# State-space mixer of an encoder layer: one segment sum and one weight matrix for both directions, double buffers, and a quarter of the out projection placed ahead of the norm

## The chip, the cores and the metric

One core of a Trainium2 chip runs the whole program. The metric is the device time of one execution in microseconds (us), here the median of several runs. Five engines work side by side, each through its own list of instructions: TensorE (PE, with its weight loads PEld), VectorE (DVE), ScalarE (ACT), GpSimd (POOL) and SyncE (SP, which starts transfers). They wait for each other on semaphores. SBUF is the main memory on the chip, PSUM (eight banks of 128 x 512 fp32) takes the results of TensorE. One fp32 matmul appears as two records in the trace.

## What is computed

An encoder of two layers over 512 tokens of width 1024. The first layer mixes the tokens by an HGRN2 recurrence and by a Mamba-2 state-space (SSD) mixer, joins both in one out projection, and then has a SwiGLU block; the second layer has an S5 mixer and a mixture of experts. The change lies in the SSD mixer and behind it. In the reference:

```python
def _ssd_one_direction(x, dt, a, bm, cm):
    ...
    acum = jnp.cumsum(dtc * a.reshape(g, hg), axis=2)
    ...
    seg = acum[:, :, :, None] - acum[:, :, None, :]
    decay = _masked_exp(mask, seg)
    cb = jnp.einsum('bclgn,bcsgn->bclsg', cc, bc)
    w = cb[..., None] * decay * dtc[:, :, None]
    y_diag = jnp.einsum('bclsgh,bcsghp->bclghp', w, xc)
    to_end = jnp.exp(acum[:, :, -1:] - acum) * dtc
    states = jnp.einsum('bclgn,bclghp->bcghpn', bc, to_end[..., None] * xc)
    ...
    y_off = jnp.einsum('bclgn,bcghpn->bclghp', cc, prev) * jnp.exp(acum)[..., None]
    return (y_diag + y_off).reshape(b, s, h, p)
```

It is called once forward and once on the flipped sequence. `d_skip` times x is added, the result is multiplied by silu(z), normalised by its mean square per group and joined with the HGRN2 output in front of `@ w_out`. There are 4 chunks of 128 tokens, 8 heads of 64 columns, 2 groups and a state of 128.

## The kernel before, in words

The program is written as one list per engine, and the order in each list is fixed by hand. Around the change the order is this.

The last projection products (`dense_fill`, L1350, handed out by `fill_to`) run on TensorE among the last pieces of the HGRN2 part; ScalarE drains their banks (L1961). VectorE runs the HGRN2 norm (`hg_finish`, L2527 reciprocal, L2529 product, L2531) and the convolution of eight blocks of columns (`convolve`, L2545 and L2549), ScalarE its silu (L2010).

Then TensorE makes the cumulative sums of dt·a by products with triangular matrices (L1431, L1432), and ScalarE their exponentials (`ex`, L2006). TensorE transposes the convolved x and B to tokens by columns (L1442), and VectorE copies these out of PSUM (L2615, L2616). GpSimd makes the weights to the chunk's end (`toend`, L1028) and x times them (`xe`, L1035, two buffers), TensorE the six state products (L1449), VectorE the running states (`Hst`; L2627 a copy, L2631 and L2633 a multiply and an add).

For each chunk c then, through one set of buffers:
- TensorE: C·B of the two groups into bank 2 (L1461); the segment sums of 8 heads and 2 directions as four products of 512 columns into banks 4 to 7 (L1468), from `dtaU`, the decays under a triangular mask (LE and GE are the two masks), which GpSimd makes (L1043).
- ScalarE: the exponential of all four banks, 128 x 2048, into `Ew` (L2016).
- VectorE: C·B under both masks (`cbm`, L2637), and `Ew` times it in four products of 128 x 512 (L2645).
- GpSimd: x times dt for both directions (`xdt`, L1049).
- TensorE: for each head and direction a product of `Ew` with `xdt`, 64 columns wide, into bank 3 (L1478, 32 records), and C times the states into banks 0 and 1 (L1484).
- VectorE: d_skip times x (L2649), the state parts scaled and added (L2654, L2656), bank 3 added (L2658), times silu(z) (L2661). ScalarE takes the squares (`ssd_squares`, L769).

After the last chunk come the square root (ScalarE, L2022), its reciprocal and the scaling (VectorE, L2663, L2668), the transposes (TensorE, L1492), and their copies into `mixT` (VectorE, L2672). Rows 0 to 3 of `mixT` hold the HGRN2 output, rows 4 to 7 the SSD output. `dense("o0", mixT)` and `dense("o1", mixT)` are the out projection, 32 matmuls each (L1179); the loop over `kk` takes rows 0 to 3 first and then 4 to 7. VectorE adds the result to the residual stream (L2680).

## Time and profile before

| | us |
|---|---|
| median of 3 runs | 2890.85 (2890.79 to 2893.72) |
| the profiled execution, its own time | 2891.91 |
| its span in the trace | 2890.1 |
| TensorE busy | 2564.2 (89%) |
| VectorE, ScalarE, GpSimd busy | 1696.9, 1250.9, 224.6 |
| first cumulative sum starts (L1431) | 452.92 |
| first exponential of segments (L2016) | 481.91 |
| out projection (L1179) | 569.15 to 624.37 |

The times of the trace count from the span's start. The profiled execution took 1.06 us longer than the median. A page of the profile gives busy times and shares; single instructions, waits and the chain that ended last come from the trace. "Clock" is the share of full speed that TensorE was granted.

### The profile page before, as it was taken

The page shows a single profiled execution, that of the slowest core. Times are in us where ns is not written, and L with a number is a line of the kernel's source. Part 1 is how long each engine was busy: PE and PEld are TensorE (multiplying, and loading weights), DVE is VectorE, ACT ScalarE, POOL GpSimd, SP SyncE. Part 2 cuts the span into 40 slices and gives each one's busy share as a digit, 9 for nine tenths or more (in the row PEclk, how much of TensorE's full clock was granted, in tenths as well). Part 3 has the DMA queues.
Part 4 walks back from the last instruction along what each step waited for, and adds up shares of the span by engine and source line. Part 5 has one row for each costly group of instructions (what it writes and reads, how often), then busy time and mean ns, then how long its engine had stood idle before and what let it go on. Part 6 is the DMA issues. An engine that isn't in the chain of part 4 may idle for free.

```text
span 2890.1 us, 31325 instructions
## 1 busy us (share of the span) xinstructions
PE 2564.2 (89%) x12573; PEld 2059.7 (71%) x12573; DVE 1696.9 (59%) x1883; ACT 1250.9 (43%) x1352; POOL 224.6 (8%) x235
## 2 busy tenths in 40 slices
PE   4989896789999997586977999999999999999977
PEld 2445564548888785486767988899779988898853
DVE  5697785422222333257336668776886778667852
ACT  2343422112222222254224657656666567556741
POOL 3003733100000000000000000000000000000010
PEclk9999988699999998757977999999999999999989
DMA  8446410013233232532317779976997789876960
GB/s 230 141 146 193 120 59 30 7 58 103 88 102 100 76 101 73 142 117 105 122 37 264 238 252 373 319 252 239 337 348 254 249 288 369 271 253 238 373 220 29
DMA packets 317023, 528.70 MB, mean 183 GB/s; under 512 B 19302, under 2 KB 175562, under 8 KB 314218
## 3 DMA queue, kind: packets, MB, share of 16 engines
q1 hardware_dynamic: 287690, 481.83, 48.9%
q0 software_dynamic: 6000, 26.27, 2.8%
q10 hardware_dynamic: 23184, 18.55, 2.0%
q8 instruction: 101, 1.65, 0.2%
q14 instruction: 48, 0.39, 0.0%
HBM read 497.05 MB, written 47.91 MB: 189 GB/s over the span
## 4 chain that ended last, share of the span: by engine, by line
PE 79%; DVE 9%; ACT 4%; issue 3%; POOL 3%; DMA 2%; SPq 0%; ACTq 0%; DVEq 0%; POOLq 0%
PE psum L1653 25%; PE psum L1281 15%; PE psum L1712 11%; PE psum L1513 5%; PE psum L1714 4%; PE psum L1179 4%; PE psum L1202 3%; PE psum L1570 2%; DVE stages_r L2909 1%; PE psum L1350 1%; PE psum L1589 1%; ACT stages_r L2153 1%; PE psum L1478 1%; POOL stages L1020 1%; DVE stages L2267 1%
## 5 line engine op out<-in xcount | busy, mean ns | idle before, releaser
L2909 DVE TENSOR_TENSOR stages_r<-kept,stages_r 128x2048 fp32r<-128x2048 f32 x336 | 769.3, 2291 | 272.6 <-ACT stages_r L2153 271.9
L1653 PE MATMUL psum<-stages_r 128*128 128x512 f32 x3136 | 749.4, 398 | 21.0 <-DVE stages_r L2964 11.1
L2153 ACT ACTIVATE stages_r<-kept 128x2048 fp32r<-128x2048 f32 x336 | 637.4, 1912 | 264.7 <-PE psum L1653 138.1
L1653 PEld LDWEIGHTS psum<-stages_r 128*128 128x128 f32 x3136 | 591.5, 191 | 148.9 <-DVE stages_r L2909 12.4
L1712 PE MATMUL psum<-stages_r 128*128 128x320 f32 x1792 | 465.8, 346 | 6.3 <-issue 3.2
L1281 PE MATMUL psum<-stages_r 128*128 128x512 f32 x1920 | 442.0, 393 | 17.2 <-DVE stages_r L2688 17.2
L1281 PEld LDWEIGHTS psum<-stages_r 128*128 128x128 f32 x1920 | 364.6, 190 | 94.0 <-issue 17.7
L1714 PE MATMUL psum<-stages_r 128*128 128x160 f32 x1792 | 423.6, 236 | 0.0
L1714 PEld LDWEIGHTS psum<-stages_r 128*128 128x128 f32 x1792 | 343.4, 192 | 2.0
L1712 PEld LDWEIGHTS psum<-stages_r 128*128 128x128 f32 x1792 | 337.7, 188 | 9.0 <-DVE stages_r L2909 3.8
L2688 DVE TENSOR_TENSOR stages_r<-kept,stages_r 128x2048 fp32r<-128x2048 f32 x54 | 123.6, 2293 | 362.6 <-ACT stages_r L2033 362.6
L2033 ACT ACTIVATE stages_r<-kept 128x2048 fp32r<-128x2048 f32 x54 | 103.1, 1915 | 349.1 <-PE psum L1281 245.1
L1513 PE MATMUL psum<-stages_r,stages_front_r 128*128 128x512 f32 x672 | 154.6, 393 | 6.8 <-DVE stages_front_r L2707 6.8
L1513 PEld LDWEIGHTS psum<-stages_r,stages_front_r 128*128 128x128 f32 x672 | 127.5, 190 | 33.9 <-issue 7.2
L1202 PE MATMUL psum<-stages,kept 128*128 128x512 f32 x256 | 119.1, 611 | 0.8 <-ACT stages L1815 0.8
L1179 PE MATMUL psum<-kept,stages 128*128 128x512 f32 x256 | 110.4, 593 | 1.6 <-ACT stages L1815 0.8
L2189 ACT ACTIVATE stages<-stages 128x160 f32<-128x160 f32 x112 | 37.8, 337 | 158.3 <-DVE stages L2941 158.3
L1179 PEld LDWEIGHTS psum<-kept,stages 128*128 128x128 f32 x256 | 48.5, 190 | 62.3 <-issue 60.3
L1086 POOL DMA_INDIRECT stages<-moe_rows_by_token,stages x8 | 18.3, 2292 | 892.6 <-PE psum L1661 522.4
L1202 PEld LDWEIGHTS psum<-stages,kept 128*128 128x128 f32 x256 | 47.2, 193 | 54.9 <-issue 53.9
L2944 DVE TENSOR_TENSOR kept<-stages 128x160 f32<-128x160 f32 x112 | 36.7, 327 | 45.2 <-ACT stages L2189 45.2
L1156 PE MATMUL psum<-kept,stages 128*128 128x128 f32 x160 | 26.1, 334 | 39.2 <-DVE stages L2267 39.0
(378 smaller groups left out, 2547.4 us busy)
## 6 DMA issues: line engine op xcount, KB each, us to landing
kept<-in_moe_w_gu_dram SPq DMA_DIRECT2D x224, 1024.0 KB, 6.2
kept<-in_moe_w_down_dram SPq DMA_DIRECT2D x112, 1024.0 KB, 6.1
kept<-in_ffn_w_gu_dram SPq DMA_DIRECT2D x28, 1024.0 KB, 5.2
kept<-in_ev_w_in_dram SPq DMA_DIRECT2D x16, 1024.0 KB, 6.7
kept<-in_ffn_w_down_dram SPq DMA_DIRECT2D x14, 1024.0 KB, 5.0
s_output_maps_by_state<-stages ACTq DMA_DIRECT2D x64, 128.0 KB, 2.0
s_input_maps<-stages ACTq DMA_DIRECT2D x32, 256.0 KB, 2.5
s_output_maps<-s_output_maps_by_state SPq DMA_DIRECT2D x32, 256.0 KB, 4.9
```

The source lines that it names most:

```text
L1179: m = pe.matmul(psum[:, b0 + b, 0:width], act[:, 4 * kk + k, b * P:(b + 1) * P], w[:, k, 0:width], **at)
L1202: m = pe.matmul(psum[:, b, :], *pair, start=kk == 0 and k == 0, stop=kk == 1 and k == 3)
L1281: m = pe.matmul(psum[:, 4 * (g % 2) + b, :], *pair, start=kk == 0 and k == 0 and n == 0, stop=kk == 1 and k == 3 and n == 2, skip_group_ch ...
L1513: m = pe.matmul(psum[:, 2 * c + hf, :], a[:, k, at], w[hf][:, k, :], start=j == 0 and k == 0 and n == 0, stop=j == FJ - 1 and k == 3 and n ...
L1570: m = pe.matmul(psum[:, b % 8, (2 * gl + e) * NC5:(2 * gl + e + 1) * NC5], w[:, 4 * i + gl, e, :], U[:, 8 * q + 4 * i + gl, :], start=True ...
L1653: m = pe.matmul(out_, a, b, start=start and n == 0, stop=stop and n == len(pairs) - 1, skip_group_check=True)
L1712: pe.matmul(bank[:, 0:2 * CAP], wh[:, k, fs], x_[:, k, :], start=k == 0, stop=False, skip_group_check=True)
L1714: m = pe.matmul(bank[:, 0:CAP], wl[:, k, fs], x_[:, k, 0:CAP], start=False, stop=k == 7, skip_group_check=True)
L2033: act.activation(f_high[t % 2], ring[:, n % RING, :].rearrange("p (k n) -> p k n", k=4), ACT.Copy).then_inc(s_wh, 1)
L2153: act.activation(w_high[n % WSLOTS], unit_tile(n), ACT.Copy).then_inc(s_wh, 1)
L2688: dve.tensor_tensor(f_low[t % 2], ring[:, (SPLIT_RUNS[run][1] + t) % RING, :].rearrange("p (k n) -> p k n", k=4), f_high[t % 2], ALU.subtr ...
L2909: dve.tensor_tensor(w_low[n % WSLOTS], unit_tile(n), w_high[n % WSLOTS], ALU.subtract).then_inc(s_ws, 1)
```

## The change

- **One segment sum for both directions.** The products for the forward and the backward direction accumulate in the same two banks; a pair of tokens lies in one triangle or in the other. The exponential is 128 x 1024 instead of 128 x 2048.
- **One weight matrix.** `Ew` is multiplied by C·B straight from PSUM (two products of 128 x 512), then by `dtw` (one of 128 x 1024). `dtw` holds dt of the forward direction under LE plus dt of the backward direction under GE; GpSimd builds it for each chunk with a multiply of 128 x 1024 and, per half, a multiply and an add of 128 x 512. The y products are then 8 matmuls (16 records), on x itself; `xdt` and `cbm` are gone. C·B is made for two chunks at a time.
- **Two buffers.** `Ew`, `dtaU`, `dtw`, `ytmp` and the banks of the segment sums are double, `xe` has six buffers. VectorE's outputs add bank 3 ahead of the state parts, so that the banks come free earlier.
- **Moved work.** The cumulative sums go ahead among the last projection products; the copies of x and B go from VectorE to ScalarE; `toend` and `xe` from GpSimd to VectorE; the HGRN2 norm of the last head goes behind the last convolution block; the state products come in another order (the forward direction first).
- **Out projection.** `dense` takes a list of halves. The HGRN2 half of `o0`, 16 matmuls, comes ahead of the transposes of the normed output, which now use banks 0 and 1; its other half and `o1` come behind them.

The diff, cut to this, with its indentation reduced:

```diff
+ytmp = [ssa.take(512) for _ in range(2)]
+Ew = [ssa.take(1024).rearrange("p (k t) -> p k t", t=P) for _ in range(2)]
...
-xe = ssa.take(1024).rearrange("p (d n) -> p d n", d=2)
...
+dtw = [ssa.take(1024).rearrange("p (k t) -> p k t", t=P) for _ in range(2)]
...
-Ew = ssa.take(2048).rearrange("p (d n t) -> p d n t", d=2, t=P)
-dtaU = ssa.take(2048).rearrange("p (d n t) -> p d n t", d=2, t=P)
+dtaU = [ssa.take(2048).rearrange("p (d n t) -> p d n t", d=2, t=P) for _ in range(2)]
+dtw_half = ssa.take(512).rearrange("p (k t) -> p k t", t=P)
...
-SSD_STATES = [(0, 0), (1, 3), (0, 1), (1, 2), (0, 2), (1, 1)]
+SSD_STATES = [(0, 0), (0, 1), (0, 2), (1, 3), (1, 2), (1, 1)]
+SSD_ENDS = [(0, 0), (0, 1), (1, 1), (0, 2), (1, 2), (1, 3)]
+SSD_SEG = lambda c: psum[:, 4 + 2 * (c % 2):6 + 2 * (c % 2), :]
+SSD_TURN = lambda c: (2, 6)[c % 2]
...
+    def masked_decays(c):
+        if c >= 2:
+            pool.wait_ge(s_seg, c - 1)
         for d in range(2):
...
+            m = pool.tensor_tensor(dtaU[c % 2][:, d, :, :], (LE, GE)[d].unsqueeze(1).broadcast_to([P, MH, P]),
                                    dta[:, d, c, :].unsqueeze(2).broadcast_to([P, MH, P]), ALU.mult)
         m.then_inc(s_dtau, 1)
...
-            m = pool.tensor_tensor(xdt[:, d, :].rearrange("p (k n) -> p k n", k=MH),
...
+    def masked_steps(c):
+        if c == 1:
+            pool.wait_ge(s_conv, CB)
+            pool.wait_ge(s_cact, 1)
+        if c >= 2:
+            pool.wait_ge(s_w, c - 1)
+        if c:
+            pool.wait_ge(s_dtw, c)
+        out_ = dtw[c % 2]
+        chain.link(pool.tensor_tensor(out_, LE.unsqueeze(1).broadcast_to([P, MH, P]),
+                                      dts[:, 0, c, :].unsqueeze(2).broadcast_to([P, MH, P]), ALU.mult))
+        for g in range(2):
+            at = slice(MH // 2 * g, MH // 2 * (g + 1))
+            chain.link(pool.tensor_tensor(dtw_half, GE.unsqueeze(1).broadcast_to([P, MH // 2, P]),
+                                          dts[:, 1, c, at].unsqueeze(2).broadcast_to([P, MH // 2, P]), ALU.mult))
+            chain.settle()
+            m = pool.tensor_tensor(out_[:, at, :], out_[:, at, :], dtw_half, ALU.add)
...
+        m.then_inc(s_dtw, 1)
+    pool.wait_ge(s_dt, 1)
+    pool.wait_ge(s_o, HEADS)
+    pool.wait_ge(s_gram, 2 * PAIR_SLOTS)
+    masked_decays(0)
+    masked_decays(1)
+    pool.wait_ge(s_X, UNITS)
+    masked_steps(0)
+    masked_steps(1)
+    for c in range(2, TC):
+        masked_decays(c)
+        masked_steps(c)
...
-    def dense(name, act):
+    def dense(name, act, halves=(0, 1)):
...
+        if g >= 2 and 0 in halves:
             all_drained(groups[g - 2][0])
...
+        for kk in halves:
...
+    fill_to(rest + 4)
...
+    pe.matmul(psum[:, 0, 128:192], ones, dta.rearrange("p d c k -> p (d c k)"), start=True,
+              stop=True).then_inc(s_cum, 1)
     hg_squares(2)
     fill_to(rest + 9)
     hg_squares(3)
     fill_to(rest + TAIL)
...
+    pe.wait_ge(s_mix, HEADS - 1)
...
     for c in range(TC):
...
+        b = SSD_TURN(c)
         if c >= 2:
...
         m.then_inc(s_xt, 1)
+    pe.wait_ge(s_ex, 1)
     for m_, (d, c) in enumerate(SSD_STATES):
...
+        pe.wait_ge(s_xtd, c + 1)
+        pe.wait_ge(s_xe, SSD_ENDS.index((d, c)) + 1)
...
         for g in range(GROUPS):
             m = pe.matmul(psum[:, m_ % 2, g * 256:(g + 1) * 256], btok[:, c, g * P:(g + 1) * P],
...
+                          xe[SSD_ENDS.index((d, c))][:, g * 256:(g + 1) * 256], start=True, stop=True)
         m.then_inc(s_st, 1)
...
+    pe.wait_ge(s_xe, 6)
     pe.wait_ge(s_cact, CB)
...
+    pe.wait_ge(s_mix, HEADS)
+    def segments(c):
+        pe.wait_ge(s_dtau, c + 1)
+        if c >= 2:
+            pe.wait_ge(s_E, c - 1)
+        for n in range(2):
+            for d in range(2):
+                m = pe.matmul(SSD_SEG(c)[:, n, :], (GT, LT)[d],
+                              dtaU[c % 2][:, d, 4 * n:4 * n + 4, :].rearrange("p k t -> p (k t)"),
+                              start=d == 0, stop=d == 1)
+        m.then_inc(s_seg, 1)
+    def cb_products(pair):
+        if pair:
+            pe.wait_ge(s_w, 2)
+        for c in (2 * pair, 2 * pair + 1):
...
+            for g in range(GROUPS):
...
+                m = pe.matmul(psum[:, 2, o:o + P], xc[:, 4 + g, at], xc[:, 6 + g, at], start=True, stop=True)
+        m.then_inc(s_cb, 1)
+    def ssd_outputs(c):
         at = slice(c * P, (c + 1) * P)
...
+        if c == 0:
+            pe.wait_ge(s_H, 6)
+        else:
             pe.wait_ge(s_yd, c)
...
         for d in range(2):
...
             for g in range(GROUPS):
                 m = pe.matmul(psum[:, d, g * 256:(g + 1) * 256], xc[:, 6 + g, at],
                               Hst[d][:, c - 1 + d, g * 256:(g + 1) * 256], start=True, stop=True)
+        pe.wait_ge(s_w, c + 1)
+        for k in range(MH):
+            m = pe.matmul(psum[:, 3, k * MP:(k + 1) * MP], Ew[c % 2][:, k, :], xst[:, c, k * MP:(k + 1) * MP],
+                          start=True, stop=True)
         m.then_inc(s_y, 1)
+    segments(0)
+    cb_products(0)
+    segments(1)
+    ssd_outputs(0)
+    segments(2)
+    cb_products(1)
+    ssd_outputs(1)
+    segments(3)
+    ssd_outputs(2)
+    ssd_outputs(3)
+    dense("o0", mixT, (0,))
     for c in range(TC):
         pe.wait_ge(s_yn, c + 1)
+        pe.wait_ge(s_yd, TC)
         if c >= 2:
             pe.wait_ge(s_ym, c - 1)
         for q in range(4):
-            m = pe.transpose(psum[:, 4 + c % 2, q * P:(q + 1) * P], yst[:, c, q * P:(q + 1) * P], ident)
+            m = pe.transpose(psum[:, c % 2, q * P:(q + 1) * P], yst[:, c, q * P:(q + 1) * P], ident)
         m.then_inc(s_yt, 1)
     pe.wait_ge(s_ym, TC)
-    dense("o0", mixT)
+    dense("o0", mixT, (1,))
...
+    act.wait_ge(s_cum, 1)
+    act.activation(ex, psum[:, 0, 0:192], ACT.Exp).then_inc(s_ex, 1)
...
+    def conv_silu(cb):
         act.wait_ge(s_conv, cb + 1)
         act.activation(xc[:, cb, :], conv[cb], ACT.Silu, bias=parT[:, 40 + cb:41 + cb]).then_inc(s_cact, 1)
+    def xs_copies(c):
+        act.wait_ge(s_xt, c + 1)
+        b = SSD_TURN(c)
+        act.activation(xst[:, c, :], psum[:, b, :], ACT.Copy)
+        act.activation(btok[:, c, :], psum[:, b + 1, 0:256], ACT.Copy).then_inc(s_xtd, 1)
+    for cb in range(4):
+        conv_silu(cb)
+    fill_drain(late[-1])
+    for cb in range(4, 7):
+        conv_silu(cb)
+    xs_copies(0)
+    conv_silu(7)
+    for c in range(1, TC):
+        xs_copies(c)
     act.activation(zs, zs, ACT.Silu).then_inc(s_zact, 1)
     for c in range(TC):
         act.wait_ge(s_seg, c + 1)
...
+        if c >= 2:
+            act.wait_ge(s_y, c - 1)
+        act.activation(Ew[c % 2].rearrange("p k t -> p (k t)"), SSD_SEG(c).rearrange("p b n -> p (b n)"),
                        ACT.Exp).then_inc(s_E, 1)
...
+        if c >= 2:
...
     convolve(CB - 2)
-    hg_finish(3)
     convolve(CB - 1)
...
-        dve.tensor_copy(xst[:, c, :], psum[:, b, :])
...
+    chain.link(dve.tensor_tensor(toend.rearrange("p d c k -> p (d c k)"), ex[:, 64:128],
...
+    chain.settle()
+    hg_finish(3)
+    def chunk_state(m_):
+        d, c = SSD_STATES[m_]
         dve.wait_ge(s_st, m_ + 1)
...
+        if m_ % 3 == 0:
             dve.tensor_copy(new, bank).then_inc(s_H, 1)
         else:
...
+            dve.wait_ge(s_H, m_)
...
             chain.settle()
...
     for c in range(TC):
...
+        for n, (d, c_) in enumerate(SSD_ENDS):
+            if c_ == c:
+                dve.tensor_tensor(heads(xe[n]), heads(xst[:, c, :]), by_head(toend[:, d, c, :]),
+                                  ALU.mult).then_inc(s_xe, 1)
+        if c:
+            chunk_state(c - 1)
+    for m_ in range(3, 6):
+        chunk_state(m_)
+    def chunk_weights(c):
+        dve.wait_ge(s_cb, c // 2 + 1)
         dve.wait_ge(s_E, c + 1)
...
+        w = Ew[c % 2]
+        for g in range(GROUPS):
+            e = w[:, HPG * g:HPG * (g + 1), :]
+            cb = psum[:, 2, (2 * (c % 2) + g) * P:(2 * (c % 2) + g + 1) * P]
+            chain.link(dve.tensor_tensor(e, e, cb.unsqueeze(1).broadcast_to([P, HPG, P]), ALU.mult))
+        dve.wait_ge(s_dtw, c + 1)
+        chain.settle()
+        dve.tensor_tensor(w, w, dtw[c % 2], ALU.mult).then_inc(s_w, 1)
+    def chunk_outputs(c):
...
         dve.wait_ge(s_xtd, c + 1)
...
+        chain.link(dve.tensor_tensor(heads(y), heads(xst[:, c, :]), by_head(dskip), ALU.mult))
         dve.wait_ge(s_y, c + 1)
         dirs = [d for d in range(2) if c != (0, TC - 1)[d]]
         for d in dirs:
...
+            chain.link(dve.tensor_tensor(heads(ytmp[d]), heads(psum[:, d, :]), by_head(exA[:, d, c, :]), ALU.mult))
         chain.settle()
         dve.tensor_tensor(y, y, psum[:, 3, :], ALU.add).then_inc(s_yd, 1)
         dve.wait_ge(s_yd, c + 1)
+        for d in dirs:
+            chain.link(dve.tensor_tensor(y, y, ytmp[d], ALU.add))
+            chain.settle()
...
         dve.tensor_tensor(y, y, zs[:, c, :], ALU.mult).then_inc(s_yz, 1)
+    chunk_weights(0)
+    chunk_weights(1)
+    chunk_outputs(0)
+    chunk_weights(2)
+    chunk_outputs(1)
+    chunk_weights(3)
+    chunk_outputs(2)
+    chunk_outputs(3)
```

**TensorE, one inner chunk.** Before, for the second chunk (L1461 is C·B, L1468 segment sums, L1478 y products, L1484 state parts):

```order
L1461 MATMUL psum<-stages 128x128 [waits cb_masked]
L1461 MATMUL psum<-stages 128x128
L1468 MATMUL psum<-stages,kept 128x512 [waits segment_exp_ready,dta_masked]
L1468 MATMUL psum<-stages,kept 128x512 x3
L1478 MATMUL psum<-stages 128x64 [waits ssd_y_drained,x_dt_ready,ssd_weights_ready]
L1478 MATMUL psum<-stages 128x64 x15
L1484 MATMUL psum<-stages 128x256 x4
```

Now, the same stretch (L1485 segment sums of the third chunk, L1498 C·B of the third and fourth, L1512 state parts and L1516 y products of the second):

```order
L1485 MATMUL psum<-stages,kept 128x512 [waits segment_exp_ready,dta_masked]
L1485 MATMUL psum<-stages,kept 128x512 x3
L1498 MATMUL psum<-stages 128x128 [waits ssd_weights_ready]
L1498 MATMUL psum<-stages 128x128 x3
L1512 MATMUL psum<-stages 128x256 [waits ssd_y_drained]
L1512 MATMUL psum<-stages 128x256 x3
L1516 MATMUL psum<-stages 128x64 [waits ssd_weights_ready]
L1516 MATMUL psum<-stages 128x64 x7
```

The segment sums of a chunk now stand ahead of the y products of the chunk before it, the state parts ahead of the y products, and of those there are 8 in place of 16.

**TensorE, end of the part.** Now, from the last y products on (L1198 is the out projection, L1537 the transposes):

```order
L1516 MATMUL psum<-stages 128x64 x7
L1198 MATMUL psum<-kept,stages 128x512 [waits ring_full0,dense_bank_drained_dve,dense_bank_drained_act]
L1198 MATMUL psum<-kept,stages 128x512 x15
L1537 MATMUL psum<-kept,stages 128x128 [waits ssd_y_drained,ssd_normed]
L1537 MATMUL psum<-kept,stages 128x128 x3
...
L1537 MATMUL psum<-kept,stages 128x128 [waits ssd_mix_ready,ssd_y_drained,ssd_normed]
L1537 MATMUL psum<-kept,stages 128x128 x3
L1198 MATMUL psum<-kept,stages 128x512 [waits ring_full1,ssd_mix_ready]
```

Before, the transposes followed the last state parts at once, and all 64 matmuls of the out projection came behind them.

**GpSimd, from the last HGRN2 work to the second chunk's masks.** Before (L1028 `toend`, L1035 `xe`, L1043 `dtaU`, L1049 `xdt`):

```order
L1028 TENSOR_TENSOR stages<-stages 128x64 [waits cumsum_exp_ready,dt_ready]
L1035 TENSOR_TENSOR stages<-stages 128x512 [waits xs_in_sbuf,to_end_ready]
L1035 TENSOR_TENSOR stages<-stages 128x512 [waits xs_in_sbuf]
L1035 TENSOR_TENSOR stages<-stages 128x512 [waits chunk_state_done,xs_in_sbuf] x4
L1043 TENSOR_TENSOR stages<-kept,stages 128x1024 x2
L1049 TENSOR_TENSOR stages<-stages 128x512 x2
L1043 TENSOR_TENSOR stages<-kept,stages 128x1024 [waits segment_sums_done]
```

Now (L1034 `dtaU`, L1048, L1052 and L1055 `dtw`):

```order
L1034 TENSOR_TENSOR stages<-kept,stages 128x1024 [waits gram_done,hg_out_done,dt_ready]
L1034 TENSOR_TENSOR stages<-kept,stages 128x1024 x3
L1048 TENSOR_TENSOR stages<-kept,stages 128x1024 [waits scaled_qk_ready]
L1052 TENSOR_TENSOR stages<-kept,stages 128x512
L1055 TENSOR_TENSOR stages<-stages 128x512 [waits pool_chain]
L1052 TENSOR_TENSOR stages<-kept,stages 128x512 [waits pool_chain]
L1055 TENSOR_TENSOR stages<-stages 128x512 [waits pool_chain]
L1048 TENSOR_TENSOR stages<-kept,stages 128x1024 [waits dt_weights_ready,conv_activated,conv_done]
```

The masks of two chunks and the first table wait only for the HGRN2 outputs and dt, no longer for the exponentials and the copies of x.

## Rows read from the trace of the kernel before

**Rows 1.** The page, busy time of each engine.
```profile
PE 2564.2 (89%) x12573; PEld 2059.7 (71%) x12573; DVE 1696.9 (59%) x1883; ACT 1250.9 (43%) x1352; POOL 224.6 (8%) x235
```

**Rows 2.** Chain of waits, second chunk and last weights: start us, us, what.
```profile
497.87 4.44 PE psum L1468 x8
...
502.33 1.89 ACT stages L2016
...
504.31 4.18 DVE stages L2645 x4
...
508.54 7.09 PE psum L1478 x32
515.63 3.52 PE psum L1484 x8
519.15 0.85 PE psum L1461 x4
520.00 3.62 PE psum L1468 x8
...
546.53 2.51 DVE stages L2645 x4
```

**Rows 3.** Chain of waits, from the last outputs to the out projection.
```profile
558.02 0.70 DVE stages L2654
...
561.85 1.28 ACT L2022
...
563.71 2.19 DVE stages L2668 x8
...
569.15 55.22 PE psum L1179 x128
```

**Rows 4.** Windows: window, length, PE, PEld, DVE, ACT, POOL busy (records), clock, DMA, GB/s.
```profile
488.00:498.00 10.00, 9.89 (x41) 9.53 (x42) 1.57 (x4) 0.00 (x0) 0.90 (x1) 0.50 0.00 0
...
580.00:600.00 20.00, 20.00 (x48) 8.92 (x47) 2.74 (x4) 0.00 (x0) 0.00 (x0) 1.00 0.25 78
```

**Rows 5.** Timeline of VectorE: start us, us, instruction.
```profile
448.00 3.35 DVE L2527 RECIPROCAL stages<-stages 128x512 f32<-128x512 f32 x1
451.38 0.69 DVE L2529 TENSOR_TENSOR stages<-psum,stages 128x512 f32<-128x512 f32 x1
452.11 0.75 DVE L2531 SCALAR_TENSOR_TENSOR stages<-stages,kept 128x512 f32<-128x512 f32 x1
...
453.30 3.11 DVE L2549 SCALAR_TENSOR_TENSOR stages<-stages,kept 128x510 f32<-128x510 f32 x4
...
520.85 0.69 DVE L2654 TENSOR_TENSOR stages<-psum,stages 128x512 f32<-128x512 f32 x1
```

**Rows 6.** Lines L2645, L1043, L1049: ns min/median/max, first and last start us, form.
```profile
L2645 DVE TENSOR_TENSOR stages<-stages x16: 679/680/2362, 483.9 to 548.3; 128x512 f32<-128x512 f32 x16
...
L1043 POOL TENSOR_TENSOR stages<-kept,stages x8: 1894/1895/2339, 473.5 to 525.5; 128x1024 f32<-128x1024 f32 x8
...
L1049 POOL TENSOR_TENSOR stages<-stages x8: 1037/1041/1489, 478.1 to 541.5; 128x512 f32<-128x512 f32 x8
```

**Rows 7.** Timeline of TensorE: last HGRN2 output product, cumulative sums.
```profile
431.04 3.60 PE L1319 MATMUL psum<-stages 128*128 128x512 f32 x8
...
452.92 1.92 PE L1431 MATMUL psum<-stages,kept 128*128 128x32 f32 x8 [5.41 <-DVE stages L2531]
454.65 0.67 PE L1432 MATMUL psum<-stages,kept 128*128 128x64 f32 x2
```

**Rows 8.** Timeline of ScalarE, last projection drain and first exponential.
```profile
447.54 0.60 ACT L1961 ACTIVATE stages<-psum 128x512 f32<-128x512 f32 x1 [5.32 <-PE psum L1350]
...
481.91 1.88 ACT L2016 ACTIVATE stages<-psum 128x2048 f32<-128x2048 f32 x1 [16.81 <-PE psum L1468]
```

**Rows 9.** Timeline of GpSimd.
```profile
455.82 0.75 POOL L1028 TENSOR_TENSOR stages<-stages 128x64 f32<-128x64 f32 x1 [56.16 <-ACT stages L2006]
...
519.23 2.49 POOL L1049 TENSOR_TENSOR stages<-stages 128x512 f32<-128x512 f32 x2 [13.10 <-PE psum L1484]
```

127 lines of the change are left out of this document (24 added, 103 removed).

## The prediction

> **What bounds the kernel now.** I read the page first: TensorE is busy for 89% of the span [rows 1], so what this change can win lies where TensorE stands idle, runs slowly or is given less to do. The chain of waits comes next, because it tells what ends last. Over the state-space part it is a ring of one chunk [rows 2]: segment sums on TensorE 4.44, the exponential on ScalarE 1.89, the four weight products on VectorE 4.18, 32 records of y products 7.09, state products 3.52, C·B products 0.85, and again. That is 22 us in which every engine waits for the one before it. The last chunk is followed by outputs, squares, square root, normalisation, transposes and copies, 11.1 us from 558.02 to 569.15, with TensorE nearly empty; after that the out projection fills it for 55.22 us [rows 3]. The windows give the clock [rows 4]: TensorE, 9.89 of 10 us busy from 488 to 498, was granted 0.50 of full speed, which is the 1.2 GHz level; in the out projection it is granted 1.00. The durations of single operations are in [rows 5] and [rows 6]. No transfer into SBUF is waited for here. Everything behind 624.37 I take as unchanged, so the sum is a shift of that moment.
>
> I cut the change into three stretches: up to the first exponential, from there to the last y product, from there to the end of the out projection.
>
> **Stretch 1, before: ends at 481.91 [rows 8].** The cumulative sums, 1.92 + 0.67 us at the lower clock [rows 7], go in between projection products where the clock is full; half of their price, 1.3 us, delays the last projection drain from 447.54 [rows 8] to about 449.1. GpSimd, which was idle for 56 us until 455.82 [rows 9], now makes four mask products (1.89 each) and the first weight table, from 434.7 on, when the last HGRN2 output product is done [rows 7]. What this does to VectorE is the question of the case. In the chain the four weight products take 4.18, but 2.51 in the last chunk [rows 2], where GpSimd has nothing left to do; the longest single one took 2362 ns against a median of 680 [rows 6], and it lasted as long as a mask product of GpSimd beside it. Against that, the product at 520.85 that reads PSUM took its usual 0.69 in the middle of GpSimd's 2.49 from 519.23 [rows 5, 9]. So I take it that a GpSimd operation and a VectorE operation with two inputs in SBUF exclude each other, each for its whole length, and one with an input in PSUM is free. GpSimd's work grows from 2 x 1.89 + 2 x 1.04 = 5.9 to 3 x 1.89 + 4 x 1.04 = 9.8 us a chunk, so this exclusion is what speaks against the change. The Trainium skill (SBUF — State Buffer, "SBUF: two separate sides") states an exclusive lock on a port pair shared by the two engines, held for a whole instruction; by this rule, the trace agrees. With the exclusion the convolution of block 7 (3.11 for its taps alone [rows 5]) ends at 456.4, the same as before, although 3.35 + 0.69 + 0.75 of the HGRN2 norm now stand behind it: the gap goes to turns with GpSimd. Then the to-end weights (64 columns, estimated at 0.25 against 0.69 for 512), this norm 4.8, and some 1.9 in which GpSimd's table for chunk 1 holds it up: 463.4. The six products x times to-end, which GpSimd did at 1.04, are on VectorE at 0.69, with two state copies of 0.69 and four pairs of multiply and add at 1.45 with issue: 11.3. The last state product does not wait for the last pair and ends at 463.4 + 11.3 - 1.45 = 473.2; four segment matmuls, one bank pair instead of two, take 8 x 0.431 = 3.44 at full clock (the out projection's records) and 0.2 to be seen: 476.8. **Gain 5.1.** The four copies of xs and B off VectorE cost nothing there; on ScalarE they are 4 x 1.0 (0.60 for a drain of 128x512 [rows 8], less for 128x256) in the shadow of VectorE's 11 us, and if that cover failed the first exponential would be at most 1 us later.
>
> **Stretch 2, before: 481.91 to 558.02, 76.1 us.** Of the ring, segment sums and the exponential halve, the y products halve, and with double buffers they need not be in one ring. TensorE's work for a chunk is then 3.4 + 0.9 + 3.5 + 3.5 at most, and ScalarE's 1.0 + 0.9; VectorE has 2 x 0.69 + 1.2 for weights and six outputs of 0.69. None comes near GpSimd's 9.8. So the longest row is GpSimd's: chunks 2 and 3 are 2 x 9.85 = 19.7 from 476.8, since the mask products of chunk 2 wait for segment sum 0. Between its operations VectorE takes its own locked ones: three of 1.2 (the 1024-wide weight product, priced by two of 0.69 less an issue) and seven of 0.69 in outputs 0 and 1: 8.5. The table of chunk 3 is ready at 476.8 + 19.7 + 8.5 = 505.0, with issue 505.2. Then weight product 1.2 and a wait of 0.3: 506.7; outputs of chunk 2 to the point where PSUM is drained, four of 0.69: 509.4; 4 state records at 0.44 and 16 y records at 0.22 at the 1.2 GHz level, 5.3, with 0.3: **515.0**, against 558.02. So 38.2 instead of 76.1, **gain 37.9**. The 0.44 and 0.22 are 3.52/8 and 7.09/32 [rows 2]. Idle gaps of about 5 us stand ahead of these records, like those ahead of the 0.50 stretch in [rows 4], so I price them at the lower level. By the Trainium skill (TensorE: Matmul & The Clock Gate, "What's actually happening") a TensorE that is kept busy is given full clock; by it these records would take half and the sum would be 2.7 us better. The row from 488 to 498 shows a busy engine at the lower level all the same, so I stay with that.
>
> **Stretch 3, before: 558.02 to 624.37, 66.35 us.** The out projection is 128 records in 55.22, that is 0.431 each [rows 3]. One quarter, 32 records of the HGRN2 half of o0, goes ahead of the norm: 13.8, plus 1.2 for a start at the lower clock (4.44 of one group of segment sums against 3.62 of a later one is 0.8; I take a little more for a longer one): 515.0 + 15.0 = 530.0. Behind it hides the tail: outputs of chunk 3 and squares 3.83 (558.02 to 561.85), table load 1.28, square root and reciprocal 0.58, normalisation 2.19 [rows 3], together 7.9, to 522.9; the cover lasts to 530.0, so even a tail 7 us longer would cost nothing. If the cover were gone, the tail would cost its 7.9. Then the transposes and their copies, which now wait for the half, 563.71 + 0.7 to 569.15, that is 4.7, and the other 96 records 41.4: 530.0 + 4.7 + 41.4 = **576.1**. It takes 61.1 instead of 66.35, **gain 5.2**; it is less than the tail because the quarter moved is longer than the tail, and the transposes stay between.
>
> **Sum.** 5.1 + 37.9 + 5.2 = 48.2 off the profiled execution's 2891.91: 2843.7. The median of the runs shown is 1.06 below that execution, so **2843** is forecast.
>
> **Rivals.**
> - *Engines that don't exclude each other, full clock.* If GpSimd and VectorE hardly hinder each other, GpSimd's 19.7 alone bounds stretch 2 and the conv gets 2 us in stretch 1; at full clock throughout, y(3) and the half gain 4 more. The out projection ends at about 560 to 562: gain 63, **2828**. For it: most L2645 records are at 680 [rows 6]. Against it: 2362 at the same place.
> - *GpSimd at its slow end, TensorE cold.* Its records reach 2339 and 1489 against 1894 and 1037 [rows 6]. At these, chunks take 13.0 instead of 9.85: 6.3 later in stretch 2 and 2 in stretch 1. Segment sums at 1.2 GHz add up to 3.4 each for one or two of them. That is 8 to 15 later: the end at 584 to 591, **2851** at its likeliest and 2858 at its edge. For it: alternating with VectorE is just when the long records occur.
> - *Slower.* The ring that was filled to one engine at a time is broken into short pieces; if TensorE is then granted 0.50 through the whole out projection, 128 records cost 0.431 more each, 55 us, and the result is +7: **2898**. It decides from 112 of the 128 records on (48.2/0.431). Against it: from 580 to 600, right behind such pieces, it is at 1.00 [rows 4], and the first half now follows more densely upon the y products.
> - *The change does nothing.* The table or the masked products would have to end up in the same ring. The order of instructions shows that they do not: segment sum 2 stands ahead of outputs 1, and the half stands ahead of the transposes.
>
> **How the numbers follow.** Forecast 0.57; no exclusion and full clock 0.13; slow GpSimd or cold TensorE 0.26; slower 0.03; nothing 0.01. A difference of 0.2%, 5.8 us, is about what a measurement of this kernel can tell from none. All of the first three are beyond it, so faster 0.95 (some 0.01 of the third falls within), same 0.02, slower 0.03. The range reaches to both neighbours: below 2828 less 2 for a tail that hides better, 2826; above 2858, where segment sums are cold as well as GpSimd slow, and again 2: 2860. Beyond it lie the slower cases and the ends of the neighbours, under 2 in 10. The two things that only this range covers are the lock's price, 8.5 us between nothing and all, and the 1024-wide operations of VectorE, which no row shows: between 0.69 and 2 x 0.69 each, 1.2 because it is a single issue.
>
> **What would show it.** GpSimd's row of the changed profile: busy without gaps of over 1.5 us from 476.8 to 505, and some 39 us in all between 434 and 505; its mask products at 1.9. VectorE: 512-wide two-input products with single records of 1.5 to 2.5 where GpSimd is at work, PSUM ones at 0.69. The chain of waits through the state-space part should pass through POOL, and TensorE's idle time in front of the y products be put down to the weight product. Out projection: 32 records, transposes, 96 records, the last ending near 576, with transposes that start at once behind the half. If GpSimd ends chunk 3 before 498 the first rival holds; after 511 the second. If the chain does not pass GpSimd in stretch 2 at all, my account of it is wrong whatever the time. If the span behind the out projection differs by over 1 us from before, the shift alone does not tell it.

## The result and the profile after

The median of the changed kernel is 2840.62 us (2838.67 to 2841.83, 4 runs) against 2892.28 (2890.79 to 2893.72, 4 runs) for the kernel before: a ratio of 0.982 with an interval of 0.9807 to 0.9832. The forecast was 2843 in a range from 2826 to 2860.

The page of the changed kernel, span and busy time, which answers to [rows 1]:

```profile
span 2839.9 us, 31193 instructions
...
PE 2539.9 (89%) x12509; PEld 2037.2 (72%) x12509; DVE 1700.9 (60%) x1870; ACT 1249.7 (44%) x1359; POOL 239.2 (8%) x240
```

TensorE is busy for 24 us less, GpSimd for 15 us more; in the other 26 us by which the span is shorter TensorE had been idle. The chain of waits of the changed kernel over the same part (start us, us, what); it answers to [rows 2] and [rows 3]:

```profile
433.98 3.43 PE psum L1338 x8
...
462.95 3.72 DVE stages L2701 x3
...
471.90 1.97 PE psum L1470 x8
473.87 3.43 PE psum L1485 x8
...
484.18 2.09 DVE stages L2719
486.27 1.67 DVE stages L2725
...
494.34 1.54 DVE stages L2719
495.87 2.30 DVE stages L2725
...
505.39 1.23 DVE stages L2719
...
509.19 2.07 PE psum L1512 x4
511.27 3.31 PE psum L1516 x16
514.58 15.38 PE psum L1198 x32
...
533.27 41.48 PE psum L1198 x96
```

Read it from the top. The last HGRN2 output product (L1338) ends at 437.41; it ended at 434.63 before [rows 7]. These 2.8 us arose ahead of the change's code, and the profiles of the experiments, in which that code is the same, put this moment anywhere from 433.5 to 438.3. So I measure the stretches from it. The ring of [rows 2] is gone: between 482.79 and 509.15 the chain is one unbroken list of VectorE, L2719 being the product with the table and L2725 the skip term. It does not pass GpSimd, although some of VectorE's operations in it are long because of GpSimd, as the rows below show.

| stretch | before | forecast | after |
|---|---|---|---|
| last HGRN2 output product to first exponential | 47.3 | 42.2 | 39.9 |
| to the end of the last y product | 76.1 | 38.2 | 37.2 |
| to the end of the out projection | 66.4 | 61.1 | 60.2 |
| sum | 189.7 | 141.5 | 137.3 |
| from there to the end of the span | 2265.7 | the same | 2265.2 |

The gain in the three stretches is 52.4 us, of which the later start takes 2.8 away.

GpSimd in the changed kernel's timeline; each row is start us, us, instruction, in brackets the idle time before it:

```profile
437.55 7.46 POOL L1034 TENSOR_TENSOR stages<-kept,stages 128x1024 f32<-128x1024 f32 x4 [36.45 <-PE psum L1338]
...
485.27 2.12 POOL L1055 TENSOR_TENSOR stages<-stages 128x512 f32<-128x512 f32 x1
...
490.14 4.65 POOL L1034 TENSOR_TENSOR stages<-kept,stages 128x1024 f32<-128x1024 f32 x2
494.76 2.87 POOL L1048 TENSOR_TENSOR stages<-kept,stages 128x1024 f32<-128x1024 f32 x1
...
501.94 1.60 POOL L1055 TENSOR_TENSOR stages<-stages 128x512 f32<-128x512 f32 x1
```

And the lines of VectorE that work beside it (ns min/median/max of one):

```profile
L2716 DVE TENSOR_TENSOR stages<-stages,psum x8: 674/676/687, 478.5 to 504.6; 128x512 f32<-128x512 f32 x8
L2719 DVE TENSOR_TENSOR stages<-stages x4: 1225/1812/2365, 479.9 to 505.4; 128x1024 f32<-128x1024 f32 x4
L2725 DVE TENSOR_TENSOR stages<-stages,kept x4: 684/1216/2378, 486.2 to 511.2; 128x512 f32<-128x512 f32 x4
L2587 DVE RECIPROCAL stages<-stages x4: 3331/3342/3354, 374.9 to 458.1; 128x512 f32<-128x512 f32 x4
```

The products that read C·B from PSUM (L2716) keep to 674 to 687 ns although GpSimd is at work beside most of them; those with both inputs in SBUF reach 1.9 times (L2719) and 3.5 times (L2725) their shortest. The 1024-wide product takes 1.23 when free, as taken. GpSimd's 14 operations of chunks 2 and 3 add up to 24.7 us where 19.7 were priced free; 0.9 of the 5.0 is that the adds (L1055) take 1.27 at best, not the 1.04 of the multiply in [rows 6]. VectorE pays more: between 482.79 and 504.01 its operations with two inputs in SBUF take 8.1 us longer than the same operations do when free (1.23 for the 1024-wide one, 0.69 for the others, 1.42 for two).

### The profile page after: what moved, and what is told of

Its sections match the earlier page's. It is cut to its first block, busy times and chain, and to the rows that moved or that the text cites. A ratio compares the mean times of both kernels' runs of the same rounds, so it can differ in the third digit from the quotient of the medians.

```text
span 2839.9 us, 31193 instructions
## 1 busy us (share of the span) xinstructions
PE 2539.9 (89%) x12509; PEld 2037.2 (72%) x12509; DVE 1700.9 (60%) x1870; ACT 1249.7 (44%) x1359; POOL 239.2 (8%) x240
## 4 chain that ended last, share of the span: by engine, by line
PE 79%; DVE 9%; ACT 3%; issue 3%; POOL 3%; DMA 2%; SPq 0%; ACTq 0%; DVEq 0%; POOLq 0%
PE psum L1698 25%; PE psum L1300 16%; PE psum L1757 11%; PE psum L1558 5%; PE psum L1759 4%; PE psum L1198 4%; PE psum L1221 3%; PE psum L1615 2%; DVE stages_r L2994 1%; PE psum L1634 1%; ACT stages_r L2213 1%; PE psum L1369 1%; POOL stages L1023 1%; POOL stages L1026 1%; PE psum L1175 1%
## 5 line engine op out<-in xcount | busy, mean ns | idle before, releaser
L1198 PE MATMUL psum<-kept,stages 128*128 128x512 f32 x256 | 112.2, 600 | 1.6 <-ACT stages L1860 0.8
L1198 PEld LDWEIGHTS psum<-kept,stages 128*128 128x128 f32 x256 | 49.1, 193 | 62.8 <-issue 60.8
```

The costliest lines, as they stand in the source:

```text
L1198: m = pe.matmul(psum[:, b0 + b, 0:width], act[:, 4 * kk + k, b * P:(b + 1) * P], w[:, k, 0:width], **at)
```

## The experiments

Differences within one part are read from the stretches, since the rest of a single profile wanders: its start by the 433.5 to 438.3 above, the part behind the out projection between 2262.4 and 2268.5 us. Where only one execution of a run was timed, its time is not used for small differences.

### More work for GpSimd, and less

Run x2, more:

```diff
-                    chain.link(pool.tensor_tensor(dtw_half, ...
-                    chain.settle()
+                    for _ in range(2 if c >= 2 else 1):
+                        chain.link(pool.tensor_tensor(dtw_half, ...
+                        chain.settle()
```

> The changed kernel with one GpSimd multiply of 128x512 more per half of the tables of chunks 2 and 3, four in all (the same product again). Theory (GpSimd's list, with the turns that VectorE takes in it, sets the end of the state-space part): the last y product is 4 x 1.04 = 4.2 to 6 us later, and the time with it. Rival (VectorE's list or the ring through the exponential sets it): under 1 us.

The stretch from the first exponential to the last y product took 39.99 us instead of 37.23: 2.8 later, between theory and rival. Its timelines tell why (GpSimd's last table, VectorE's wait for it):

```profile
506.13 1.26 POOL L1056 TENSOR_TENSOR stages<-stages 128x512 f32<-128x512 f32 x1
```

```profile
504.32 1.28 DVE L2717 TENSOR_TENSOR stages<-stages,psum 128x512 f32<-128x512 f32 x2 [0.28 <-ACT stages L2076]
507.43 1.23 DVE L2720 TENSOR_TENSOR stages<-stages 128x1024 f32<-128x1024 f32 x1 [1.83 <-POOL stages L1056]
```

Now VectorE does wait for GpSimd, 1.83 us. Counted from the first exponential, the last table came at 30.76 instead of 26.20, 4.6 later as the theory has it (the other 1.0 of the 2.8 is that VectorE itself came later: its operations ahead of this one were held longer, and it waited 0.28 for an exponential); but in the changed kernel it had lain ready 1.9 us before VectorE came to use it (503.54 against 505.39). So GpSimd's list was not the last there; VectorE's was, by 1.9 us.

Run x3, less:

```diff
             for c in range(2, TC):
                 masked_decays(c)
-                masked_steps(c)
...
-                dve.wait_ge(s_dtw, c + 1)
+                dve.wait_ge(s_dtw, min(c + 1, 2))
```

> GpSimd builds no tables of dt for chunks 2 and 3; these chunks use the tables of chunks 0 and 1. That leaves out 12.2 us of GpSimd's 19.7 in the stretch. Theory: VectorE's own list becomes the bound, and with its operations at their free durations the last y product comes 8 to 10 us earlier. Rival (something else ends last in the stretch): under 2 us.

The stretch took 30.67 us, 6.6 less. VectorE's operations of chunk 2 have their free durations here (of this run's timeline):

```profile
487.69 1.23 DVE L2718 TENSOR_TENSOR stages<-stages 128x1024 f32<-128x1024 f32 x1
488.84 0.69 DVE L2724 TENSOR_TENSOR stages<-stages,kept 128x512 f32<-128x512 f32 x1
```

One operation ahead of them has not: the product with the table of chunk 1, which lies beside the mask products (L1034) that GpSimd still makes in this run.

```profile
480.29 2.73 DVE L2718 TENSOR_TENSOR stages<-stages 128x1024 f32<-128x1024 f32 x1
```

That is 1.5 us over its free 1.23. So VectorE's own list, with the waits for the first two chunks and the last y products, is 30.7 less 1.5, that is 29.2 us long. What it shares with GpSimd adds 8.1 in the changed kernel, of which this run takes 6.6 away. The theory had 8 to 10, which leaves out the masks; the rival is out.

### Which operations exclude each other

Run x4:

```diff
-                dve.tensor_tensor(w, w, dtw[c % 2], ALU.mult).then_inc(s_w, 1)
+                dve.tensor_scalar(w, w, 0.5, None, ALU.mult).then_inc(s_w, 1)
...
-                    chain.link(dve.tensor_tensor(y, y, ytmp[d], ALU.add))
+                    chain.link(dve.tensor_scalar(y, y, 0.5, None, ALU.mult))
```

and the skip term and the product with silu(z) in the same way.

> In the chunks' weights and outputs VectorE's operations with two inputs in SBUF (times the table, skip term, adding the state parts, times silu(z)) become operations with one input and a constant, as many and as wide; this leaves out those terms of the result. GpSimd's work and all waits stay. Theory (only operations with two SBUF inputs exclude GpSimd's): GpSimd's 10 operations of chunks 2 and 3 take their free 19.7 us, no VectorE operation is stretched, and the last y product comes 5 to 8 us earlier. Rival (no exclusion; long records have another cause): under 2 us, what the shorter operations themselves give, and GpSimd's records keep their 1.3 to 2.9 us.

The stretch took 32.98 us, 4.3 less, under the theory's 5 to 8, and about 3.7 of the 4.3 is that the operations with one input are shorter by themselves: what sharing adds to VectorE's list is 7.5 us here, against 8.1. Only the stretch is read: with other values the part behind it took 2821 us instead of 2265. So the time alone does not decide against the rival; the rows do. Also the operations with one input are not left alone (VectorE of this run):

```profile
L2725 DVE TENSOR_SCALAR stages<-stages x4: 420/950/2114, 483.9 to 505.0; 128x512 f32<-128x512 f32 x4
L2737 DVE TENSOR_SCALAR stages<-stages x4: 427/898/2003, 488.0 to 511.1; 128x512 f32<-128x512 f32 x4
```

The longest takes five times the shortest, beside a GpSimd operation of 2.3 us. GpSimd's operations (14, not 10 as the expectation counts them) took 22.0 instead of 24.7, not the free 19.7. My form of the rule, two inputs in SBUF and no others, falls: this fast one-input form, 420 ns for 512 columns against 690 for the two-input ones, is held too, and the reciprocal, one input and 3.3 us, is not. The Trainium skill (SBUF — State Buffer, "SBUF: two separate sides") names both kinds, VectorE operations with two SBUF inputs and those in a two-port performance mode; this run agrees with the second, which I had left out.

### The half of the out projection

Run x1:

```diff
-            dense("o0", mixT, (0,))
...
-            dense("o0", mixT, (1,))
+            dense("o0", mixT)
```

> The changed kernel, but all 64 matmuls of the out projection behind the transposes, as before. From the last y product to the last record of the out projection the change takes 60.2 us. Theory (the quarter moved ahead covers the tail of the last chunk): the tail, some 6 to 7 us from the last y product to the first normed chunk, lies open again, so 65 to 67 us, and the time is 5 to 7 us longer, 2846 to 2848. Rival (the tail is short and the moved quarter only waits elsewhere): within 1.5 us of the change.

From the last y product to the end of the out projection it took 66.33 us instead of 60.17: 6.2 more. The median was 2849.5 (2848.15 to 2850.63), 8.9 above the change's, more than the 5 to 7 expected; the stretch holds 6.2 of it. The other 2.7 I cannot place: in the one profile the part behind the out projection, whose work this edit does not touch, is 3.1 us longer, which is within the spread given above.

Run x5, the same part alone on the kernel before:

```diff
+            pe.wait_ge(s_E, TC)
+            dense("o0", mixT, (0,))
             for c in range(TC):
                 pe.wait_ge(s_yn, c + 1)
+                pe.wait_ge(s_yd, TC)
...
-            dense("o0", mixT)
+            dense("o0", mixT, (1,))
```

> The kernel before with one part of the change: the HGRN2 half of o0 ahead of the transposes, which go to banks 0 and 1. Theory (the half covers the tail after the last y products and nothing else changes): from the last state product's end to the out projection's end 60 to 61.5 us instead of 66.35, and the time 5 to 6.5 us below before. Rival (the half needs the other parts of the change to be worth anything, since the tail here is longer by the state parts' additions): under 2 us.

Its chain of waits:

```profile
555.38 1.81 PE psum L1484 x4
557.20 15.39 PE psum L1179 x32
572.59 0.45 PE psum L1495 x4
...
575.91 41.48 PE psum L1179 x96
```

The end is at 617.39, 60.2 us behind the last state product, as forecast. The median was 2885.11 (2883.2 to 2889.1, 10 runs) against 2892.41, 7.3 lower where 5 to 6.5 were expected, a ratio of 0.9977 (0.9967 to 0.9986). The 6.2 us do not depend on the rest of the change. The start of the moved quarter costs about the same too: 32 records take 15.39 here and 15.38 in the changed kernel, against 13.8 at full clock; in the other runs that keep them in one piece behind the last y products it was 14.9 to 16.2.

### Two buffers or one

Run x6:

```diff
-        Ew = [ssa.take(1024).rearrange("p (k t) -> p k t", t=P) for _ in range(2)]
+        Ew = [ssa.take(1024).rearrange("p (k t) -> p k t", t=P)] * 2
...
-            chunk_weights(0)
-            chunk_weights(1)
-            chunk_outputs(0)
...
+            for c in range(TC):
+                chunk_weights(c)
+                chunk_outputs(c)
```

with `dtw`, `dtaU`, the segment banks and the other engines' lists likewise.

> The changed kernel with one buffer each of the exponentials, the masked products, the tables and the segment banks, and each engine's list in the order of chunks (weights and outputs of a chunk together). Work is the same. Theory (the double buffers let GpSimd make chunk 1's products ahead of the first exponential): GpSimd has three chunks of 9.8 us behind it instead of two, and TensorE's, ScalarE's and VectorE's steps lie in a ring again: the first exponential is 0 to 4 us earlier, the last y product 10 to 14 us later. Rival (the smaller work of a chunk gives the gain by itself): the last y product within 3 us.

The first exponential came 36.9 us after the last HGRN2 output product, 3.0 earlier; the last y product 46.5 after that instead of 37.2. So it is 6.3 later in all, and the one run took 2846.83. The theory's direction holds, its 10 to 14 do not: in the ring GpSimd and VectorE meet less often. A chunk of GpSimd's operations takes 10.8 to 11.4 us here, against 11.5 and 13.2 in the changed kernel. Of its chain of waits:

```profile
488.86 3.68 PE psum L1514 x16
```

The y products of three chunks, with TensorE idle for 3.2 to 4.5 us before them, are at 0.23 us a record here; those of chunk 2, with 2.4 us idle before them, are at 0.12. Of the 38.9 us that the change took out of the second stretch, 29.6 are there with single buffers too (76.1 to 46.5): the smaller work of a chunk together with its changed order inside a chunk, which I did not try apart. The other 9.3 come with the second buffers, which cost 3.0 in the first stretch.

### The moves in the first stretch

Run x10:

```diff
             convolve(CB - 2)
+            hg_finish(3)
             convolve(CB - 1)
...
-            hg_finish(3)
```

> The changed kernel with the last head's HGRN2 norm ahead of the last convolution block, as before the change. Work is the same. From the last HGRN2 output product to the first exponential the change takes 39.92 us. Theory (the norm's 3.35 us reciprocal takes nothing that GpSimd holds, so its place decides how much of GpSimd's first tables VectorE pays for; but the last silu and three pairs of copies on ScalarE then wait for the later convolution): the stretch takes 1 to 4 us more. Rival (VectorE's sum is the same in either order, and it is VectorE's sum that counts): within 0.5 us.

The stretch took 44.95 us instead of 39.92, 5.0 more. The products x times to-end show where (VectorE of this run, then of the changed kernel):

```profile
461.25 5.48 DVE L2701 TENSOR_TENSOR stages<-stages 128x512 f32<-128x512 f32 x3
```

```profile
458.08 3.35 DVE L2587 RECIPROCAL stages<-stages 128x512 f32<-128x512 f32 x1
...
462.86 3.80 DVE L2701 TENSOR_TENSOR stages<-stages 128x512 f32<-128x512 f32 x3
```

In the changed kernel GpSimd's table for chunk 1, released by the last convolution, begins at 457.99, and the reciprocal lies over it. With the norm ahead, the same table starts when the products x times to-end do, and these three take 5.48 instead of 3.80. By the last of the six products the delay is 2.7 us, inside the theory's 1 to 4. The other 2.3 are TensorE's. Its last state products stand behind a longer gap, and it runs them at a granted clock of 0.50 instead of 1.00 (this run, then the changed kernel):

```profile
471.88 5.46 PE L1470 MATMUL psum<-stages 128*128 128x256 f32 x12 [2.50 <-DVE stages L2701]
```

```profile
470.54 1.10 PE L1470 MATMUL psum<-stages 128*128 128x256 f32 x4 [0.51 <-DVE stages L2701]
471.90 1.97 PE L1470 MATMUL psum<-stages 128*128 128x256 f32 x8 [0.27 <-DVE stages L2695]
```

The total is more than the theory's; the rival is out.

Run x11:

```diff
             fill_to(rest + TAIL)
+            pe.wait_ge(s_gdr, 2 * PAIR_SLOTS)
...
+            fill_drain(late[-1])
+            act.wait_ge(s_cum, 1)
+            act.activation(ex, psum[:, 0, 0:192], ACT.Exp).then_inc(s_ex, 1)
```

> The changed kernel with the cumulative sums behind the last projection product again, and their exponential on ScalarE behind the last projection drain, all silus behind it, as before the change. From the last HGRN2 output product to the first exponential the change takes 39.92 us. Theory (the early sums cost 1.1 us ahead of the last drain and save ScalarE a table load and keep the silus and the transposes early): the last convolution 1.1 us earlier, transposes 4 to 6 us later, of which VectorE's norm covers most; in all between 1 us less and 3 us more. Rival (what stretch 1 gained, it gained by the earlier sums): 5 us or more.

41.23 us, 1.3 more than the change, inside the theory's range; the rival is out. But the 1.3 is not time that the sums save. The last eight records of the state products start 34.1 us after the last HGRN2 output product, 0.4 earlier than in the changed kernel; then they and the first segment sums run partly at the lower clock:

```profile
470.05 3.28 PE L1470 MATMUL psum<-stages 128*128 128x256 f32 x8 [0.27 <-DVE stages L2693]
```

They take 3.28 instead of 1.97, and the segment sums 3.81 instead of 3.43. So of the moves tried, the norm's place matters (2.7, and 2.3 of clock that came with it), the early sums gave nothing that these two profiles show, and GpSimd's work ahead for chunk 1 takes 3.0. The stretch's 7.4 can be read from the rows as well. Before, the first segment sums stood 3.5 us behind the last state product, which ended at 474.69; TensorE waited for the running states and for GpSimd's mask:

```profile
477.14 0.71 PE L1461 MATMUL psum<-stages 128*128 128x128 f32 x4 [2.44 <-DVE stages L2633]
478.17 3.70 PE L1468 MATMUL psum<-stages,kept 128*128 128x512 f32 x8 [0.32 <-POOL stages L1043]
```

Now they follow at once, at 473.87, and take 3.43. That is 3.5 and 0.3 of the 7.4; the other 3.6 is that the last state product ends 36.5 us after the last HGRN2 output product instead of 40.1. How much of this the copies on ScalarE and the products on VectorE gave I did not try.

### Better than the change

TensorE idles in front of the segment sums of chunk 3 and, for 5.3 us, in front of the last y products. The moved quarter can be put there, run x7:

```diff
             ssd_outputs(1)
+            pe.wait_ge(s_E, 3)
+            dense("o0", mixT, (0,), (0,))
             segments(3)
             ssd_outputs(2)
+            dense("o0", mixT, (0,), (1,))
             ssd_outputs(3)
-            dense("o0", mixT, (0,))
+            dense("o0", mixT, (0,), (2, 3))
```

> The changed kernel with the moved quarter cut by banks: bank 4 of o0 between the y products of chunk 1 and the segment sums of chunk 3, bank 5 between the y products of chunks 2 and 3, banks 6 and 7 behind the last y products. Theory (TensorE idles 1.8 and 5.3 us there, for VectorE; work put there is free, and the clock stays up, so that the last y products take 0.11 us a record instead of 0.21): the last y product 2 to 3 us earlier, then 6.9 us of out projection instead of 15.4, transposes when the norm is ready, end of the out projection 9 to 11 us earlier, time 2829 to 2832. Rival (the clock falls all the same and the bank 4 piece holds up chunk 3): 5 to 7 us earlier.

TensorE's timeline of this run:

```profile
501.74 3.65 PE L1198 MATMUL psum<-kept,stages 128*128 128x512 f32 x8
507.22 1.13 PE L1512 MATMUL psum<-stages 128*128 128x256 f32 x4 [1.83 <-DVE stages L2734]
508.19 1.89 PE L1516 MATMUL psum<-stages 128*128 128x64 f32 x16
509.92 7.08 PE L1198 MATMUL psum<-kept,stages 128*128 128x512 f32 x16
...
520.76 43.16 PE L1198 MATMUL psum<-kept,stages 128*128 128x512 f32 x96 [0.78 <-DVE stages L2760]
```

The windows give the clock, first of the changed kernel, then of this run (window, length, busy time of PE, PEld, DVE, ACT, POOL, clock, DMA, GB/s):

```profile
509.00:514.50 5.50, 5.30 (x21) 4.95 (x22) 2.82 (x5) 0.91 (x4) 0.00 (x0) 0.50 0.00 0
```

```profile
503.00:510.00 7.00, 5.17 (x27) 3.44 (x26) 6.70 (x10) 0.69 (x4) 0.00 (x0) 1.00 0.20 70
...
521.00:531.00 10.00, 10.00 (x20) 4.25 (x20) 1.38 (x2) 0.00 (x0) 0.00 (x0) 0.83 0.05 18
```

With the work in the gap TensorE keeps its full clock, and the last y products take 0.12 us a record instead of 0.21. The second stretch is 2.5 us shorter, the third 6.3: 8.8, a little under the theory's 9 to 11, since the last 96 records took 43.16 instead of 41.48: in their first 10 us the clock was 0.83. Why is open. The idle time around the transposes alone is not it, for x9 and x12 below have the same and took 41.47; they lack the 1.83 us of idle time in front of the last state parts. The median is 2832.3 (2831.64 to 2833.69), a ratio of 0.9793 (0.9776 to 0.9809).

Run x9 adds to that:

```diff
+                for d in range(2):
+                    for k in range(MH):
+                        m = act.activation(dtaU[c % 2][:, d, k, :], (LE, GE)[d], ACT.Copy, scale=dta[:, d, c, k:k + 1])
...
             for c in range(2, TC):
-                masked_decays(c)
                 masked_steps(c)
```

> As the run with the quarter cut by banks, and the masked products of chunks 2 and 3 are made by ScalarE (32 copies of 128x128 with a scale per token) instead of GpSimd. Theory (VectorE's list, stretched by what it shares with GpSimd, ends the stretch; ScalarE shares nothing with it): GpSimd has 12.2 us in the stretch instead of 19.7, the last y product another 4 to 6 us earlier, and the out projection with it, time 2824 to 2828. Rival (ScalarE's 32 small instructions, 4 us a chunk, hold up the exponentials): no gain over the other run, or up to 3 us of loss.

2828.84 (2826.23 to 2829.4), just above the 2824 to 2828 expected. The second stretch became 1.7 us shorter, not 4 to 6; the third became 1.7 shorter as well, since the last 96 records kept full clock. ScalarE's timeline:

```profile
476.72 4.77 ACT L2078 ACTIVATE stages<-kept,stages 128x128 f32<-128x128 f32 x16
481.40 1.00 ACT L2086 ACTIVATE stages<-psum 128x1024 f32<-128x1024 f32 x1
```

The second exponential stood behind sixteen copies of 0.30 us, and VectorE waited 2.96 us for it. That is the rival's mechanism, at a part of its price. Run x12 answers it:

```diff
+            masked_decays(1)
...
+                if c == 0:
+                    masked_decays(2, (0,))
+                if c == 1:
+                    masked_decays(2, (1,))
+                    masked_decays(3, (0,))
```

> As the run with the quarter cut by banks and ScalarE's masked products for chunks 2 and 3, with two changes: ScalarE also makes chunk 1's, in its idle time ahead of the first exponential, and its products for chunks 2 and 3 are cut by direction, so that the second and the third exponential do not wait for 16 of them. Theory: GpSimd is 3.8 us less in VectorE's way among the convolutions, first exponential 2 to 3 us after the last HGRN2 product earlier; the second exponential is not held up (1.5 us); time 2823 to 2827. Rival (VectorE's list in the first stretch is bound by its own work and ScalarE's copies): within 1 us of that run.

2827.36 (2825.31 to 2828.88), a ratio of 0.9773 (0.9757 to 0.979), which lies clear of the change's 0.9807 to 0.9832; 2823 to 2827 were expected. The first stretch took 37.73, 2.2 less as expected. The second hardly moved, 32.81 against 32.99: the second exponential came in time, but then GpSimd held the product of chunk 1 with its table to 2.30. Against the run before, the medians differ by 1.5 us and their ranges overlap.

## Why the prediction was right, and where it was not

**The ring and its end.** The gain was placed in the second stretch, 37.9 us; it was 38.9. The ring broke up as said. One reading is wrong: "segment sums and the exponential halve". The segment sums of a chunk are four products of 512 columns before and after (x8 in [rows 2], 3.62 us); they only need half the banks. The sum priced them at 3.44, so it did not suffer.

**What ends last there.** The step "So the longest row is GpSimd's" failed. The sum counted GpSimd's 19.7 and VectorE's locked 8.5 and left out VectorE's operations on PSUM, because they can lie beside GpSimd; but they stand in VectorE's list, and that list was the longer by 1.9 us. By its own test, a chain that passes GpSimd, the account was wrong; x2 and x3 show what holds instead: VectorE's list of 29.2, plus 8.1 from sharing. That the number came near is luck, because two errors cancel. The last table was forecast 28.4 us after the first exponential and was ready at 26.2, because VectorE's locked operations made GpSimd's own only 4.1 longer instead of 8.5 (with 0.9 for the adds and 1.5 of gaps that is the 26.2); VectorE was taken to be there by then, and came at 28.05. Two more of the signs named ahead went the other way: TensorE's 5.3 us of idle time before the last y products is put down to VectorE's output (L2731), not to the weight product, and GpSimd's operations between 434 and 505 add up to 47 us, not some 39.

**The exclusion.** Right in the main. Its price of 8.5 was close in size and charged to the wrong list: it is VectorE's that grew by 8.1. Its form, "two inputs in SBUF", was too narrow, as x4 shows.

**The first stretch.** Forecast gain 5.1, measured 7.4. Counted from the last HGRN2 output product, the norm was done at 25.5 instead of 28.8. Two terms were mis-sized: 1.9 us of this is the time for which GpSimd's table for chunk 1 was to hold the norm, whose last step fell between two of its operations and took its 0.75; another 1.3 is that the last convolution ended at 20.5 instead of 21.8. The steps after the norm gave 1.0 back.

**The clock.** The last y products were taken at the lower level because of the idle time before them: 0.21 us a record at a granted clock of 0.50, as forecast. The three others had at most 1.6 us of idle time straight ahead of their group and were at 0.12. So what decided in this kernel was what TensorE did just before, and x7 changes it from one to the other. The forecast looked for this only at the last y products; x10 and x11 show that it moves the first stretch as well, by 2.3 and 1.7 us. The rule that a TensorE kept busy has full clock (the Trainium skill, TensorE: Matmul & The Clock Gate, "What's actually happening") agrees with x7; the busy stretch at 0.50 from 509.0 on shows that it need not have it at once.

**The third stretch.** Forecast gain 5.2, measured 6.2. The moved quarter took 15.4, against 15.0. Transposes and copies took 3.3 us (529.95 to 533.27) instead of 4.7, since all but the first are overlapped; the cover was 7 us too long, as said, and x7 uses that.

**The rivals.** None came true. Against full clock and no exclusion speak the windows at 0.50 and the records of 2.4 us; the slow end had GpSimd's durations nearly right (24.7 us for chunks 2 and 3, against its 26), but they are long because they wait for VectorE, so VectorE's turns don't come on top: the last table was ready 26.2 us after the first exponential, where this rival needed 34.7, and the first two segment sums ran at full clock (3.43 and 3.45). The 96 records of the out projection took 41.48, which is full clock, against the slower result. The part behind the out projection did not move: 2265.2 against 2265.7.

## What to carry to other kernels

Where two engines exclude each other, write down both lists with all their instructions, the free ones too, and let the longer of them set the end; what was made cheaper on TensorE here, by a table built on GpSimd, was paid in part on VectorE, which lost 8.1 us. Build ahead while the neighbour runs something that shares nothing: here one reciprocal over GpSimd's table was worth 2.7 us, and 5.0 with what TensorE's clock made of the delay. Put ready matmuls into TensorE's gaps and not in one block behind them: in x7 they filled the gap, and the last y products behind them ran at full clock.

## What was not expected of the hardware

A VectorE operation with one input, in its fast form of 420 ns for 128x512, took up to 2.1 us beside GpSimd, while a reciprocal of 3.3 us ran beside GpSimd with neither of the two stretched. ScalarE makes a 128x128 product with a scale per token in 0.30 us, 4.8 us for 16, beside both engines: slower than GpSimd's 3.75 for the same chunk, but in nobody's way.
